# A causal mask in sparse attention: from TensorE mask products to VectorE's add-and-minimum

## The reference, cut to what matters

```
logits = q_rope[i] @ k[0 .. i].T / 8          # keys of blocks 0 to i only
logits = where(key <= query, logits, -1e30)   # matters in the diagonal block alone
p      = exp(logits - max(logits)); p = p / sum(p) * gate
out   += p @ v[0 .. i]
```

## Time and profile before

| what | us |
|---|---|
| median of three runs | 2032.55 |
| the profiled execution | 2032.62 |
| its span, first to last instruction | 2030.8 |
| TensorE busy | 2010.4 (99%) |
| VectorE busy | 1463.7 (72%) |
| ScalarE busy | 971.6 (48%) |

### The profile page before, as it was taken

One profiled execution on the slowest core, in us unless ns is written; L12 is line 12 of the kernel. 1 busy time (PEld: TensorE's weight loads), 2 busy tenths in 40 slices (PEclk: granted clock), 3 DMA queues, 4 the chain that ended last, 5 costly groups with the idle time before them and its releaser, 6 DMA issues.

```text
span 2030.8 us, 26501 instructions
## 1 busy us (share of the span) xinstructions
PE 2010.4 (99%) x10076; PEld 1616.8 (80%) x10076; DVE 1463.7 (72%) x2141; ACT 971.6 (48%) x1659; POOL 56.5 (3%) x100
## 2 busy tenths in 40 slices
PE   9999999999999999999999999999999999999998
PEld 7888778788888887777778888888777777777787
DVE  7788899777776347888777776447787758566664
ACT  5577775344443226777654444224443332444531
POOL 0000001000000001111000000000000000000000
PEclk9999999999999999999999999999999999999999
DMA  5322222222332333211223332333222224111132
GB/s 179 122 74 73 73 73 74 92 95 93 94 102 85 92 112 114 63 63 42 83 94 94 102 93 85 105 97 103 83 83 73 78 78 166 53 53 53 53 104 83
DMA packets 56223, 179.43 MB, mean 88 GB/s; under 512 B 6287, under 2 KB 9487, under 8 KB 55992
## 3 DMA queue, kind: packets, MB, share of 16 engines
q1 hardware_dynamic: 52416, 167.80, 26.6%
q10 hardware_dynamic: 3704, 10.30, 1.5%
HBM read 175.95 MB, written 4.74 MB: 89 GB/s over the span
## 4 chain that ended last, share of the span: by engine, by line
PE 87%; DVE 8%; ACT 2%; issue 1%; DMA 1%; DVEq 0%
PE bankpair L300 25%; PE bankpair L304 25%; PE bankpair L301 25%; DVE conv_rows L402 1%; PE bankpair L1555 1%; PE bankpair L1587 1%; PE bankpair L1567 1%; PE bankpair L741 1%; DVE weights_low L335 1%; PE bankpair L1423 1%; PE bankpair L1411 1%; PE bankpair L762 1%; DVE padded_rows L2596 1%; DVE arena L2688 0%; DVE arena L2703 0%
## 5 line engine op out<-in xcount | busy, mean ns | idle before, releaser
L300 PE MATMUL bankpair<-scaled_in_high,weights_high 128*128 128x512 f32 x1856 | 743.7, 401 | 1.5 <-DVE scaled_in_low L2652 0.5
L301 PE MATMUL bankpair<-scaled_in_low,weights_high 128*128 128x512 f32 x1856 | 723.5, 390 | 0.0
L324 ACT ACTIVATE weights_high<-weight_ring 128x1024 fp32r<-128x1024 f32 (+3 forms) x344 | 333.9, 972 | 340.6 <-DMA weight_ring<-down_dram 149.3
L304 PE MATMUL bankpair<-scaled_in_high,weights_low 128*128 128x512 f32 x1856 | 462.9, 389 | 0.0
L335 DVE TENSOR_TENSOR weights_low<-weight_ring,weights_high 128x1024 fp32r<-128x1024 f32 (+3 forms) x344 | 384.7, 1127 | 54.3 <-ACT weights_high L324 44.7
L300 PEld LDWEIGHTS bankpair<-scaled_in_high,weights_high 128*128 128x128 f32 x1856 | 348.7, 188 | 83.2 <-issue 6.3
L301 PEld LDWEIGHTS bankpair<-scaled_in_low,weights_high 128*128 128x128 f32 x1856 | 348.8, 188 | 75.7 <-issue 5.7
L304 PEld LDWEIGHTS bankpair<-scaled_in_high,weights_low 128*128 128x128 f32 x1856 | 348.4, 188 | 72.5
L300 PE MATMUL bankpair<-gated_high,weights_high 128*128 128x512 f32 x448 | 175.1, 391 | 1.9 <-DVE gated_low L2652 1.2
L301 PE MATMUL bankpair<-gated_low,weights_high 128*128 128x512 f32 x384 | 149.4, 389 | 0.0
L593 DVE TENSOR_TENSOR padded_rows<-bankpair,inv_rms 128x512 f32<-128x512 f32 x88 | 60.8, 691 | 106.4 <-PE bankpair L304 106.1
(11 more groups left out here) (428 smaller groups left out, 2418.8 us busy)
## 6 DMA issues: line engine op xcount, KB each, us to landing
weight_ring<-up_dram SPq DMA_DIRECT2D x88, 512.0 KB, 3.5
weight_ring<-w_in_dram SPq DMA_DIRECT2D x70, 512.0 KB, 3.5
weight_ring<-in_w_dram SPq DMA_DIRECT2D x40, 512.0 KB, 3.5
weight_ring<-down_dram SPq DMA_DIRECT2D x32, 384.0 KB, 3.1
weight_ring<-kvq_dram SPq DMA_DIRECT2D x24, 512.0 KB, 3.5
weight_ring<-down_dram SPq DMA_DIRECT2D x32, 320.0 KB, 2.9
weight_ring<-out_a_dram SPq DMA_DIRECT2D x8, 512.0 KB, 3.5
weight_ring<-out_b_dram SPq DMA_DIRECT2D x8, 512.0 KB, 3.6
```

The source lines that it names most:

```text
L300: nc.tensor.matmul(bank, WH[:, high_slot, cell], high, start=(k == 0), stop=False)
L301: nc.tensor.matmul(bank, WH[:, high_slot, cell], low, start=False, stop=False)
L304: mm = nc.tensor.matmul(bank, WL[:, slot, cell], high, start=False, stop=(c == last_k))
L324: nc.scalar.activation(WH[:, (PART0[name] + k) % SLOTS, 0:n], RAW[:, b % SLOTS, 0:n], ACT.Copy).then_inc(high_ready, 1)
```

## The change

The masks by TensorE go, and with them the two bf16 constants. Each part and group has one product for its scores, of (i + 1) x 128 columns. DVE's `maxima` becomes `logits`: for each part and group one `tensor_tensor_reduce` reads the bank, adds a row `FUTURE_ROW` (zeros for 384 columns, then the mask's 128; the end of it is taken that fits the part's length), multiplies by -1 and writes to `PB`, with the minimum of what it wrote beside it, which is the negated maximum. ACT takes the exponentials in place in `PB` with a factor of -1. The scores of a turn now wait for DVE's logits of the turn before, no longer for ACT's exponentials, and the wait for a free `PB` moves from ACT to DVE. `FUTURE_ROW` is the buffer `reciprocals`; DVE fills it ahead of the compressed branch's logits.

```diff
--- before.py
+++ after.py
@@ -113,8 +113,7 @@
         PAR = sb("params", [P, PARAM[None]])
         ONES = sb("ones", [P, P])
         FLAT = sb("small_buffers", [P, 400])
-        ONEHOT = sb("identity_for_one_pass", [P, P], BF16)
-        FUTURE = sb("future_for_one_pass", [P, P], BF16)
+        MINUS = sb("minus_one", [P, 1])
         EPSC = sb("eps_column", [P, 1])
         KCBOTH = sb("compressed_keys_both", [P, 64])
         UNUSED = sb("unused_exp", [P, 1 + LINE_FILL])
@@ -1275,6 +1274,7 @@
         VSUM = FLAT[:, 212:212 + 2 * NT].rearrange("p (e c) -> p e c", c=NT)
         ROWPICK = FLAT[0:96, 208:210].bitcast(BF16)
         EM, RDEN, HG = EMB[:, :], RDB[:, :], STD[:, 0:P]
+        FUTURE_ROW = RDB[:, :]
         flat = FLAT[:, :]
         GK = flat[:, 0:16].rearrange("p (c h) -> p c h", h=4)
         GN = flat[:, 16:112].rearrange("p (c h) -> p c h", h=24)
@@ -1440,7 +1440,7 @@
                 nc.tensor.transpose(BANK[6][:, 32 * c:32 * c + 4], GR[0:4, tok], IDENT[0:4, 0:4])
                 mm = nc.tensor.transpose(BANK[5][:, 32 * c:32 * c + 24], GR[64:88, tok], IDENT[64:88, 64:88])
             mm.then_inc(gT_done, 1)
-            pe.wait_ge(masks_set, 6)
+            pe.wait_ge(masks_set, 5)
             for h in range(MH):
                 m = HT * (h + 1)
                 spread(h)
@@ -1541,19 +1541,13 @@
                 j, _ = nsa_step(w)
                 pe.wait_ge(roped, 6)
                 if w >= 1:
-                    pe.wait_ge(n_p, nsa_exps(w))
-                parts = nsa_at(w)
-                for i, _, at in parts:
+                    pe.wait_ge(n_l, w)
+                for i, c, at in nsa_at(w):
+                    n = (i + 1) * P
                     for g in range(2):
-                        nc.tensor.matmul(BANK[2 + g][:, at + i * P:at + (i + 1) * P], ONEHOT[:, :], FUTURE[:, :],
-                                         start=(at == 0), stop=False)
-                for i, c, at in parts:
-                    for keys in (slice(i * P, (i + 1) * P), slice(0, i * P))[0:1 + (i > 0)]:
-                        last = (i, c, at) == parts[-1] and keys.start == 0
-                        for g in range(2):
-                            half = slice(64 * g, 64 * g + 64)
-                            mm = nc.tensor.matmul(BANK[2 + g][:, at + keys.start:at + keys.stop],
-                                                  QR[half, j, i * P:(i + 1) * P], (KS, KW)[c][half, keys], start=False, stop=last)
+                        half = slice(64 * g, 64 * g + 64)
+                        mm = nc.tensor.matmul(BANK[2 + g][:, at:at + n], QR[half, j, i * P:(i + 1) * P], (KS, KW)[c][half, 0:n],
+                                              start=True, stop=True)
                 mm.then_inc(n_s, 1)
 
             def nsa_turn(w):
@@ -1820,13 +1814,11 @@
 
             def exps(w):
                 act.wait_ge(n_l, w + 1)
-                if w >= 2:
-                    act.wait_ge(n_t, w - 1)
                 for x, (i, _, at) in enumerate(nsa_at(w)):
                     n = (i + 1) * P
                     for g in range(2):
-                        nc.scalar.activation(PB[w % 2][:, g, at:at + n], BANK[2 + g][:, at:at + n], ACT.Exp,
-                                             bias=NM2[w % 2][:, g, x:x + 1],
+                        p = PB[w % 2][:, g, at:at + n]
+                        nc.scalar.activation(p, p, ACT.Exp, bias=NM2[w % 2][:, g, x:x + 1], scale=-1.0,
                                              accum_out=SM2[w % 2][:, g, x:x + 1]).then_inc(n_p, 1)
 
             def turned(w):
@@ -1895,10 +1887,9 @@
 
         def second_dve(dve, step, rs, hr, fr, cv):
             gr = Count(dve, g_row)
-            nc.vector.tensor_copy(ONEHOT[:, :], IDENT).then_inc(masks_set, 1)
+            nc.vector.memset(MINUS[:, :], -1.0).then_inc(masks_set, 1)
             nc.vector.memset(ROWPICK, 0.0).then_inc(masks_set, 1)
             dve.wait_ge(masks_set, 2)
-            nc.vector.tensor_copy(FUTURE[:, :], const("future_neg")).then_inc(masks_set, 1)
             for i in range(3):
                 nc.vector.tensor_copy(ROWPICK[32 * i:32 * i + 4, :], IDENT[32 * i:32 * i + 4, 32 * i:32 * i + 4]).then_inc(masks_set, 1)
             dve.wait_ge(gemm_done, TILE0["gates_w"] + 1)
@@ -2087,6 +2078,8 @@
             seen = const("cmp_seen").rearrange("p (i n) -> p i n", n=NCMP)
             never = const("cmp_neg").rearrange("p (i n) -> p i n", n=NCMP)
             step.step(nc.vector.memset(CL, 0.0))
+            step.step(nc.vector.memset(FUTURE_ROW[:, 0:T - P], 0.0))
+            step.step(nc.vector.tensor_copy(FUTURE_ROW[:, T - P:T], const("future_neg")))
             step.step(nc.vector.tensor_tensor(GN[:, :, 0:24:3], GN[:, :, 0:24:3],
                                               seen[:, :, 0:1].to_broadcast([P, NT, 8]), ALU.mult))
 
@@ -2110,12 +2103,19 @@
                 step.step(nc.vector.tensor_tensor(CSM, CSM, GN[:, :, 3 * j:3 * j + 13:12], ALU.mult))
                 cp.step(nc.vector.tensor_tensor(CL, CL, CSM.unsqueeze(3).to_broadcast([P, NT, 2, 32]), ALU.mult))
 
-            def maxima(w):
+            def logits(w):
+
                 parts = nsa_at(w)
+                if w >= 2:
+                    dve.wait_ge(n_t, w - 1)
                 dve.wait_ge(n_s, w + 1)
                 for x, (i, _, at) in enumerate(parts):
-                    (nl if x == len(parts) - 1 else step).step(nc.vector.tensor_reduce(
-                        NM2[w % 2][:, :, x], BANKPAIR[1][:, :, at:at + (i + 1) * P], AX.X, ALU.max, negate=True))
+                    n = (i + 1) * P
+                    for g in range(2):
+                        last = g and x == len(parts) - 1
+                        (nl if last else step).step(nc.vector.tensor_tensor_reduce(
+                            PB[w % 2][:, g, at:at + n], BANK[2 + g][:, at:at + n], FUTURE_ROW[:, T - n:T], MINUS[:, 0:1],
+                            3e38, ALU.add, ALU.min, NM2[w % 2][:, g, x:x + 1]))
 
             def probs(w):
 
@@ -2158,7 +2158,7 @@
                 if w == NSA_STEPS:
                     low_a(KD // 2, KD)
                 if w < NSA_STEPS:
-                    maxima(w)
+                    logits(w)
                 if w == NSA_STEPS - 1:
                     low_a(0, KD // 2)
                 if w % NTURNS == 4 and NTURNS < w < NSA_STEPS:
```

## The result

The changed kernel takes 2041.05 us, the median of six runs (2040.54 to 2041.79), where the kernel before takes 2032.49 beside it: a ratio of 1.0042, between 1.0032 and 1.0052. It is 8.6 us slower. The forecast was 2029.4, and its range ended at 2031.0. The profiled execution has a span of 2039.3 us, 8.5 more than before, at the same granted clock (0.998). The chain that ended last has the same shares as in the earlier trace rows.

A forecast was written before the change was run, and what follows sets the result against it. TensorE, busy throughout the changed stage, was taken as the bound. 3.9 + 0.2 + 0.25 - 0.7 - 0.0 - 0.5 = 3.2 us off 2032.62 gave 2029.4, range 2028.1 to 2031.0.

The forecast's parts named there:

- the one that opens the sum: Total taken as TensorE's gain over 20 sparse-attention turns, corrected at three places where it waits, or nearly, for DVE.
- The masks: Sparse attention: without mask products TensorE gains 0.24 us in 12 turns, 0.13 in 8; 3.9 in all.
- Merging: Scores of the sparse attention: one product in place of two gains 0.2 us, between 0 and 0.5.
- Logits on DVE: Sparse attention: 11.3 us more DVE work, hidden by one turn's slack of 3.9 us; ACT's exponentials 0.04 longer each.
- Turn 0: Start of sparse attention: memset and copy delay TensorE's L1537, loss 0.7 us (0.55 to 0.85); later transposes lose nothing.
- Last turn: End of sparse attention: longer logits delay DVE's low parts, and TensorE loses 0.5 us, between 0.3 and 0.7.
- Start of the second block: Two DVE conversions fewer ahead of the first tile's bank: TensorE gains 0.25 us, between 0.2 and 0.3.
- rival 4: Middle turns: DVE becomes the bound if its new operation takes four times as long; 2041 us, chance 0.03.
- Rivals 1 to 3 and 5: Edges free, 2028.2 (chance 0.11); masks worth 5.7, 2027.6 (0.04); masks free, 2032.9 (0.06); 5: some mask or second products left.

The follow-up runs named there:

- the old places: The changed kernel with the column of -1 widened to 128 columns, so every later SBUF tensor lies where it lay before the change: 2030.16 us, ratio 0.9988.
- the hole of 32 bytes: The kernel before with only an unused tensor of 32 bytes ahead of `eps_column`, moving all tensors behind it: 2043.34 us, ratio 1.0053.
- the kernel with 64 bytes: The kernel before with only an unused tensor of 64 bytes ahead of `eps_column`: 2036.64 us, ratio 1.0020.
- the hole of 128 bytes: The kernel before with only an unused tensor of 128 bytes ahead of `eps_column`: 2042.9 us, ratio 1.0050.

## Why the prediction was wrong, point by point

- **The step that failed is the one that opens the sum**: I added up what the changed instructions do, and took the products that the diff doesn't name as untouched. The two lines of the diff on `ONEHOT` and `FUTURE` were read as two constants less, not as 480 bytes less ahead of three operands of TensorE. The instruction lists show that nothing else moved in TensorE's order; where its operands lie they don't show. By the mean distances, 1872 products of 512 columns on `gated`, `head_out` and `query_in` cost 11.6 us more in all; the two medians, with and without the old places, differ by 10.9. No rival and no bound of the range had such a term. It is shown by undoing it alone and by doing it alone.
- **The masks**: 0.24 and 0.13 a turn, 3.9 in all. Turns 1 to 17 (11 of them with two parts, 6 with one) should win 11 x 0.24 + 6 x 0.13 = 3.4 by it, and with the merged products 3.6; the tiles' ends come 3.6 nearer. Right. The gap of 0.09 in front of the scores stays, which the rule on draining (the Trainium skill, page "TensorEngine Tiling (Array Packing)", section "Key Properties") says too: 0.54 from two products to the scores here, not 0.45. No run here tells a drain from other causes of this gap.
- **Merging**: right in size, and too small to be read by itself but for the turns with block 1, whose scores take 1.064 us in place of 1.092, from their first start to the start of what follows.
- **Logits on DVE**: pairs of 0.79 for 512 columns as forecast (0.395 for 128, 0.66 for 384), and no wait of TensorE for them in turns 1 to 18. ACT's exponential of 512 columns takes 716 ns from SBUF, forecast 715.

```profile
L2116 DVE CUSTOM_DVE_ANT_0 arena<-bankpair,reciprocals,minus_one 128x512 f32<-128x512 f32 x16 | 12.0, 748 | 0.3
```

```profile
L1821 ACT ACTIVATE arena<-arena 128x512 f32<-128x512 f32 x16 | 11.4, 716 | 17.5 <-DVE arena L2116 17.5
```

- **Turn 0**: the right wait, but too small. L1537 was to start 0.7 later behind the scores, between 0.55 and 0.85. It started 1.07 behind them in before and starts 1.93 behind them in the changed kernel and 1.89 with the old places, so 0.86 and 0.82 later (the waits are 0.80 and 0.75). The forecast took 0.67 for what the two instructions add, and they delay the next one by 0.79. The transposes of turn 0 are reached with 0.21 of slack, so they cost nothing, as forecast.
- **Last turn**: 0.5 forecast, 0.76 - 0.28 = 0.48 measured. Right.
- **Start of the second block**: 0.25 forecast; the lag falls by 0.21 there. Right. In the version with the old places it is 0.13, since the memset of the wider column takes 0.17 and not 0.06.
- **The rivals**: rival 4 named nearly the measured time, 2041, but its mechanism did not occur: DVE's new operation has the duration of the earlier trace rows, and TensorE waits for none of it in the middle turns. A time that fits is no evidence for the cause that it was computed from. Its sum is off besides: at four times the logits of a two-part turn take 8.4 us, with the exponentials 7.2 more than before, which is 3.3 over the slack of 3.9 and not about 1; some three times would give that. Rivals 1 to 3 and 5 fall with the rows above.

With the old places the forecast would have been near: its terms, less 0.1 for the wider memset, are 3.1 us, and the span of that kernel is 2028.0, 2.8 less than before. Its profile is 0.14 late at the first tile and 0.19 at 653 us, ahead of any changed instruction, as that of the changed kernel is by 0.49 at the first tile (I put both down to scatter, and did not test it). Its median, 2030.16, is 2.4 below that of before.

## What to carry to other kernels

A diff that adds or removes a buffer changes more than its instructions: everything placed behind it moves. Where that changed how operands of TensorE lie to the weights, it alone was worth 0.2% to 1.3% here, while the edit itself was worth 0.1%; where all moved together it cost nothing. Compare the SBUF places of all large operands before and after, and when one operand of TensorE has moved against the weights, keep the old places by padding before you judge the edit. The old places are the reference for the comparison and not the best ones for every shape: see the products of 256 columns below. A loss spread thinly over stages without a changed line, in groups with equal counts and a mean some ns longer, is the sign of it.

## What the runs showed of the hardware

- An fp32r product of 512 columns takes 227 ns from start to start when moving operand and weights leave the same rest by 256 bytes, 229 at a difference of 64 bytes, and 232 to 234 at the other multiples of 32 that were tried; 16 bytes gave 232 and 4 bytes 237. Series of two-pass fp32 and of bf16 products, tried at 0 and 32 bytes, showed nothing of it (41.4 us for both series; 216 ns).
- With 256 columns it is not so. The last projection has 96 fp32r products of 256 columns on `gated`, and their mean distance is 119.7 ns in before, 116.8 with the hole of 32 bytes, 114.3 with 64 and 119.7 with 128. The same rest by 256 is the slowest place here, tied with 128. The groups of before and of the kernel with 64 bytes:

```profile
L1652 PE MATMUL bankpair<-gated_low,weights_high 128*128 128x256 f32 x32 | 8.0, 288 | 0.0
```

```profile
L1653 PE MATMUL bankpair<-gated_low,weights_high 128*128 128x256 f32 x32 | 7.7, 282 | 0.0
```

- It goes by the difference, not by the place: all moved by 32 bytes, 2032.44 us; `gated` alone, 2043.34; the weights and `gated` by 128 bytes against `scaled_in`, 2059.75.
- Open: what in TensorE or SBUF makes the two places meet. The reading of the next weights during a product is a candidate. No run isolates it, but the traces speak for it. In 20 places a product on `scaled_in`, whose own operands have not moved, is followed by one whose weights lie in `arena`: the distance goes from 228.3 ns to 233.3, 226.8 and 233.4 with holes of 32, 64 and 128 bytes. Where only the next product's moving operand has moved (`gated` behind `scaled_in`, 9 places) it stays at 227.
- Open, too, is why 64 bytes are a middle case and -64 not, and why `scaled_in_low` lost only 3.3 ns where `scaled_in_high` lost 7.0 with the same weights. The difference modulo 256 is not the whole of it: `gated_low` lost 6.3 ns with the hole of 128 bytes, at the same difference modulo 256 at which `scaled_in_low` lost 3.3.
